# Hybrid decoder layer: inverse products one to three issued in a row, and convolution steps moved into the recurrence

## What is computed

```python
h = einsum('btd,dc->btc', x, w_in)
qa, ka, va, za, ba, aa, qb, kb, vb, zb = split(h, offsets)
ya = _deltanet_group(qa, ka, va, za, ba, aa, conv_w, a_log, dt_bias, norm_w)
yb = _swa_group(qb, kb, vb, zb, sinks)
y = einsum('btc,cd->btd', concatenate([ya, yb]), w_out)
x = layernorm(2 ** 0.25 * x + y) * ln_g + ln_b
```

## Time and profile before

| | |
|---|---|
| median of 3 runs | 1091.87 us (1090.0 to 1093.45) |
| the profiled execution | 1090.27 us, its span 1088.5 us |
| TensorE matmuls busy | 1064.2 us, 98% of the span |
| TensorE weight loads busy | 846.5 us, 78% |
| VectorE busy | 688.7 us, 63% |
| ScalarE busy | 532.7 us, 49% |
| GpSimd busy | 115.9 us, 11% |
| mean granted TensorE clock | 0.999 |
| HBM read and written | 138.22 and 44.07 MB |

### The profile page before, as it was taken

The page is one execution under the profiler, slowest core; times in us unless marked ns, Lnnn a source line. Parts: engine busy times, 40 slices in busy tenths (PEclk is TensorE's granted clock), DMA queues, the critical chain, the costliest instruction groups (busy, mean ns, idle before and its releaser), DMA issues.

```text
span 1088.5 us, 19513 instructions
## 1 busy us (share of the span) xinstructions
PE 1064.2 (98%) x7212; PEld 846.5 (78%) x7212; DVE 688.7 (63%) x2081; ACT 532.7 (49%) x1557; POOL 115.9 (11%) x152
## 2 busy tenths in 40 slices
PE   7999999999999999999999999999999999999997
PEld 5877787778778787777887878787787878787885
DVE  5285959584665747576365665757537575758565
ACT  4557675754636454363354535435344555564300
POOL 3413132134100000020000000002000000002210
PEclk9999999999999999999999999999999999999999
DMA  8967475665553626253562551715454343622432
GB/s 282 315 209 262 163 274 195 243 208 183 201 205 109 237 73 235 87 185 98 175 228 93 165 215 46 265 49 185 132 179 157 126 157 128 215 73 63 137 116 77
DMA packets 58430, 183.55 MB, mean 169 GB/s; under 512 B 8480, under 2 KB 21216, under 8 KB 45024
## 3 DMA queue, kind: packets, MB, share of 16 engines
q1 hardware_dynamic: 58192, 182.05, 48.7%
q10 hardware_dynamic: 144, 0.26, 0.1%
HBM read 138.22 MB, written 44.07 MB: 167 GB/s over the span
## 4 chain that ended last, share of the span: by engine, by line
PE 65%; DVE 6%; DMA 2%; issue 1%; ACT 0%; SPq 0%; DVEq 0%
PE bank L849 33%; PE bank L900 10%; PE bank L1137 4%; PE bank L957 2%; PE bank L990 2%; PE bank L972 2%; PE bank L1107 1%; PE bank L1120 1%; PE bank L1117 1%; PE bank L1121 1%; DVE y_cols L1797 1%; DVE y_step L1793 1%; PE bank L1030 1%; PE bank L1045 1%; PE bank L1115 1%
## 5 line engine op out<-in xcount | busy, mean ns | idle before, releaser
L849 PE MATMUL bank<-xr,w 128*128 128x512 f32 x2496 | 653.9, 405 | 7.4 <-DVE xr L1534 7.4
L849 PEld LDWEIGHTS bank<-xr,w 128*128 128x128 f32 x2496 | 449.8, 189 | 101.7 <-issue 9.8
L900 PE MATMUL bank<-wo,y_split 128*128 128x512 f32 x432 | 114.4, 404 | 0.0
L900 PEld LDWEIGHTS bank<-wo,y_split 128*128 128x128 f32 x432 | 77.0, 189 | 14.6 <-issue 0.7
L1582 DVE SCALAR_TENSOR_TENSOR kq<-conv_in,convw_all,kq 128x512 f32<-128x512 f32 x96 | 77.3, 806 | 7.8 <-ACT conv_in L1191 5.8
L1487 ACT ACTIVATE o_scaled<-bank 128x128 f32<-128x128 f32 x64 | 17.7, 277 | 124.5 <-PE bank L1121 124.3
L1353 ACT ACTIVATE score<-score,neg_max 128x256 f32<-128x256 f32 (+1 forms) x128 | 62.7, 493 | 29.0 <-DVE neg_max L1759 29.0
L1919 DVE TENSOR_SCALAR steps<-bank,nb_rk 128x128 f32<-128x128 f32 x64 | 22.3, 348 | 63.9 <-PE bank L1117 63.9
L1922 DVE SCALAR_TENSOR_TENSOR state<-state,cols_all,bank 128x128 f32<-128x128 f32 x64 | 22.2, 347 | 63.2 <-PE bank L1120 63.2
L1793 DVE TENSOR_TENSOR y_step<-blocks,y_cols 128x60 f32<-128x60 f32 (+14 forms) x240 | 50.3, 210 | 12.1 <-DMA blocks<-n_spill 3.3
L783 POOL TENSOR_TENSOR xr<-y_tile,xr 128x256 fp32r<-128x256 f32 x8 | 6.0, 774 | 455.1 <-ACT xr L1172 455.1
(11 more groups left out here) (217 smaller groups left out, 1628.3 us busy)
## 6 DMA issues: line engine op xcount, KB each, us to landing
w<-w_split SPq DMA_DIRECT2D x78, 1024.0 KB, 5.4
w_split<-w SPq DMA_DIRECT2D x26, 1024.0 KB, 5.1
blocks<-n_spill SPq DMA_DIRECT2D x32, 256.0 KB
y_spill<-y_out SPq DMA_DIRECT2D x30, 256.0 KB, 5.8
x_tile<-w_in SPq DMA_DIRECT2D x13, 512.0 KB, 6.1
y_tile<-w_in SPq DMA_DIRECT2D x12, 512.0 KB, 6.4
y_tile<-y_spill SPq DMA_DIRECT2D x12, 512.0 KB, 6.1
x_tile<-x SPq DMA_DIRECT2D x12, 512.0 KB, 3.9
```

What stands on the lines that cost most here:

```text
L849: ins = nc.tensor.matmul(bank[JOBS[at].bank][:], w[:, turn % 3, wp, k, :], xr[:, xp, k], start=(step == 0), stop=(step == 3 * KT - 1))
L900: ins = nc.tensor.matmul(bank[JOBS[at].bank][:], y_place(t)[:, yp, k], wo[:, k, wp, half * UNIT:(half + 1) * UNIT], start=(step == 0), sto ...
```

## The change

On TensorE, product 1 comes directly behind the dense steps of `p16`; then follow the second scores, product 2, the first values and product 3, with no dense steps between them. `Places` loses `p32`, and the others move: `p16` by +0.3 of a level, `y16` (still used by VectorE and ScalarE) to 1.6 levels, `y32` to 2.8. A level is 4 to 7 dense steps.

On VectorE, the transpose of product 2 stands directly behind the copy of product 1. Behind it come `gate_b`, the copies into `t32`, the finished output jobs, the weight or `split_y` and only then the maxima. On ScalarE the copies of products 2 and 3 stand before all exponentials of the second half.

The convolution is counted in single taps, 9 a slot, where it was counted in halves. From slot 3 on (`n >= AH - 1`) none is done ahead of the base inverses; one tap may follow the maxima, q's three taps are completed after `divide`, and the other six are handed out one at a time in the recurrence of chunks 0 and 1, behind `resid`, behind `v_new` and behind `state`. `slopes` moves to chunk 2 there. In slots 0 to 2 what `convs` does ahead of the base inverses stays, and the rest comes in one block after `divide` as before.

```diff
-        self.p16, self.y16, self.p32, self.y32, self.p64 = (first + level * a for a in range(5))
+        self.p16, self.y16, self.y32, self.p64 = (first + level * a for a in (0.3, 1.6, 2.8, 4))
...
                 fill_to(n, at.turns0)
                 turns(n, 0)
                 fill_to(n, at.p16)
-                values(n, 0)
                 after(pe, t_ready, n, 1)
                 after(pe, pt_ready, n, 2)
                 quads_of(lambda c, rows: nc.tensor.matmul(quad_place(bank[6], rows, c), n_t[rows, c, rows], t0[rows, c],
                                                           start=True, stop=True)).then_inc(inv_done.sem, 1)
                 scores(n, 1)
-                fill_to(n, at.y16)
                 after(pe, r_ready, n, 1)
                 after(pe, v_tok_ready, n, CH)
                 quads_of(lambda c, rows: nc.tensor.matmul(quad_place(bank[4], rows, c), r16[rows, c], y0[rows, c],
                                                           start=True, stop=True)).then_inc(inv_done.sem, 1)
-                fill_to(n, at.p32)
+                values(n, 0)
                 after(pe, t_ready, n, 2)
                 pairs_of(lambda c, one, two: nc.tensor.matmul(quad_place(bank[6], two, c), n_t[one, c, two], t16[one, c],
                                                               start=True, stop=True)).then_inc(inv_done.sem, 1)
...
                 after_jobs(n, at.p16)
                 after(act, t_ready, n, 2)
                 nc.scalar.activation(y16, quad_tiles(bank[4]), ACT.Copy).then_inc(inv_copied.sem, 1)
-                weights(n, 1, (0,))
+                take(p32, quad_tiles(bank[6]), 3)
+                weights(n, 1)
                 after_jobs(n, at.y16)
-                take(p32, quad_tiles(bank[6]), 3)
-                weights(n, 1, (1,))
                 after(act, inv_copied, n, 1)
                 for b in range(4):
                     rows = slice(b * QUAD, (b + 1) * QUAD)
                     nc.scalar.activation(y_inv[rows, :, rows], y16[rows], ACT.Copy)
                 if n == SLOTS - 1:
                     round_y(11)
-                after_jobs(n, at.p32)
+                after_jobs(n, at.y16)
...
-            def conv(m, c, half):
+            def conv(m, c, step):
...
-                if half == 0:
+                if step == 0:
                     after(dve, raw_copied, m, c + 1)
                     after(dve, tail_put, m, 1)
-                for step in (0,) if half == 0 else (1, 2):
-                    if step > 0:
-                        after(dve, conv_step, m, 2 * c + step)
-                    ins = nc.vector.scalar_tensor_tensor(acc, conv_in[:, c, step:step + UNIT],
-                                                         convw_all[:, i, c, step:step + 1], acc, ALU.mult, ALU.add)
-                    ins.then_inc(conv_step.sem if step < CONV - 2 else conv_ready.sem, 1)
-                if c == 2 and half == 1:
+                else:
+                    after(dve, conv_step, m, 2 * c + step)
+                ins = nc.vector.scalar_tensor_tensor(acc, conv_in[:, c, step:step + UNIT],
+                                                     convw_all[:, i, c, step:step + 1], acc, ALU.mult, ALU.add)
+                ins.then_inc(conv_step.sem if step < CONV - 2 else conv_ready.sem, 1)
+                if c == 2 and step == CONV - 2:
                     nc.vector.tensor_copy(tails[:, i], conv_in[:, :, UNIT:]).then_inc(tail_saved.sem, 1)
                     if m < SLOTS - 1:
...
-            def convs(n, f, most=6):
-
-                while conv_place[0] < 6 * SLOTS and most > 0:
-                    m, part = divmod(conv_place[0], 6)
-                    c, half = divmod(part, 2)
+            def convs(n, f, most=9):
+
+                while conv_place[0] < 9 * SLOTS and most > 0:
+                    m, part = divmod(conv_place[0], 9)
+                    c, step = divmod(part, 3)
                     if JOBS[JOB_AT["qkv"[c], m]].end > n + f + 1e-6:
                         return
-                    conv(m, c, half)
+                    conv(m, c, step)
                     conv_place[0] += 1
                     most -= 1
+
+            def conv_gap(n, f):
+
+                if n >= AH - 1:
+                    convs(n, f, 1)
...
-                convs(n, 0.2)
+                if n < AH - 1:
+                    convs(n, 0.2)
                 after_jobs(n, at.base)
                 if n == SLOTS - 1:
                     split_y(9)
                 base_inverses(n)
-                after_jobs(n, at.p16)
+                if n < AH - 1:
+                    after_jobs(n, at.p16)
                 after(dve, inv_done, n, 1)
                 nc.vector.copy_predicated(r16[:], lower16[:].rearrange("p b c -> p (b c)").unsqueeze(1).to_broadcast([P, CH, QUAD]),
                                           quad_tiles(bank[6])).then_inc(r_ready.sem, 1)
-                gate_b(n, 0)
-                if t is not None and i < AH - 1:
-                    split_y(t)
-                else:
-                    convs(n, 0.34, 1)
-                maxima(n, 1)
                 after(dve, inv_done, n, 2)
                 nc.vector.transpose(t16, quad_tiles(bank[4])).then_inc(t_ready.sem, 1)
+                gate_b(n, 0)
                 after(dve, t_ready, n, 2)
                 for b in range(2):
                     rows = slice(b * QUAD, (b + 1) * QUAD)
                     nc.vector.tensor_copy(t32[rows, :, rows], t16[rows])
+                after_jobs(n, at.p16)
+                if n < AH - 1:
+                    weight_rest(n, "k")
+                if t is not None and i < AH - 1:
+                    split_y(t)
+                maxima(n, 1)
+                if n >= AH - 1 and (t is None or i == AH - 1):
+                    convs(n, 0.34, 1)
                 if t is not None and i == AH - 1:
                     normalise(n, at.y16)
-                if n < AH - 1:
-                    weight_rest(n, "k")
-                after_jobs(n, at.p32)
+                after_jobs(n, at.y16)
                 if n < AH - 1:
                     convs(n, 0.34, 1)
                 after(dve, inv_done, n, 4)
                 nc.vector.transpose(t32[QUAD:HALF, :, 0:QUAD], quad_tiles(bank[5])[0:QUAD]).then_inc(t_ready.sem, 1)
                 divide(n, 1)
-                if n < SLOTS - 1:
+                if n < AH - 1:
                     slopes(n + 1)
                 if i == AH - 1 and s < SBS - 1:
                     after_jobs(n, JOBS[JOB_AT["bT", s + 1]].end - n)
                 if n == SLOTS - 1:
                     split_y(10)
                     split_y(11)
-                convs(n, at.p32)
+                convs(n, at.y16, 9 if n < AH - 1 else max(0, 9 * (n + 1) + 3 - conv_place[0]))
                 after_jobs(n, at.step0)
...
                     nc.vector.scalar_tensor_tensor(resid, bank[4][:, 0:P], col(EG)[:, one], v_tok[:, c], ALU.mult, ALU.subtract)\
                         .then_inc(resid_ready.sem, 1)
                     after_jobs(n, at.chunk(c, 1 / 3))
+                    conv_gap(n, at.p64 if c == 0 else at.chunk(c - 1))
                     after(dve, tr_done, n, c + 1)
                     nc.vector.tensor_scalar(v_new, bank[6][:, 0:P], nb_rk[:, one], None, ALU.mult).then_inc(v_new_ready.sem, 1)
                     after_jobs(n, at.chunk(c, 2 / 3))
+                    conv_gap(n, at.p64 if c == 0 else at.chunk(c - 1))
                     after(dve, kv_done, n, c + 1)
                     nc.vector.scalar_tensor_tensor(state[:, i], state[:, i], col(EGT)[:, one], bank[4][:, P:2 * P],
                                                    ALU.mult, ALU.add).then_inc(state_ready.sem, 1)
                     if n == SLOTS - 1 and c < 3:
                         split_y(12 + c)
                     after_jobs(n, at.chunk(c, 0.8))
-                    if c < 3:
-                        convs(n, (at.p64, at.chunk(0), 1)[c], 1 if n == AH - 1 and c < 2 else 6)
+                    if n < AH - 1:
+                        if c < 3:
+                            convs(n, (at.p64, at.chunk(0), 1)[c])
+                    elif c < 2:
+                        convs(n, (at.p64, at.chunk(0))[c], 1)
+                    elif c == 2:
+                        convs(n, 1)
+                        if n < SLOTS - 1:
+                            slopes(n + 1)
                     if c == CH - 1:
                         if t is not None and i == AH - 2:
                             split_y(t + 1)
```

## The result

The changed kernel takes 1098.94 us, median of six runs (1097.53 to 1104.37). The kernel before, run beside it on the same chip, takes 1091.64 us (1090.0 to 1095.61). The ratio is 1.008, with a 95% interval of 1.0059 to 1.0101: slower by 0.8%. The profiled execution took 1097.64 us with a span of 1095.9 us, 7.4 us more than the span before.

What follows compares the result with a forecast made beforehand. TensorE, 98% busy in matmuls, was taken as the bound. Terms -7.1 + 3.3 + 0.6 + 1.1 + 3.1 + 3.9 + 2.4 = +7.3 us gave 1097.6 from the profiled 1090.27, 1099 against the runs' median; 8-in-10 range 1091 to 1103.5.

Steps and rivals of the forecast that it cites:

- Seams: TensorE between products 1 and 4: two dense runs gone as runs, 0.22 us each, saving 0.44 us a slot, 7.1 in 16.
- Product 1's waits: Slots 0 to 3, 7, 11, 12: product 1 comes earlier but `t0` no sooner, so 3.3 us given back; bounds 0 and 4.5.
- `turns(n, 1)`: Slots 4, 5, 8, 9, 12 to 14: later second-half attention on VectorE uses up the slack; some 0.1 us each, 0.6 in all.
- `split_y` in slots 6 and 10: The o0 job starts five dense steps behind product 3 and needs `split_y`, which ends later: 2 x 0.55 = 1.1 us.
- Slots 0 to 2: VectorE, the tight engine there, idles and makes `resid` and L1117 late: 1.05 us each, 3.1 in all; ends 1.5 and 5.
- the third idle time: Slots 0 to 2: VectorE idle 0.9 us ahead of `divide`, as the weight's low part stands before the maxima.
- Chunk 1's tap: Slots 4, 5, 6, 8, 9, 10: a tap between `add_half` and `v_new` costs 6 x 0.75 = 4.5 us, net 3.9.
- Slot 15: The `after_jobs` of `p16` now stands before the maxima, delaying `split_y(10)` and chunk 1's `resid`: 2.4 us; ends 0 and 3.5.

## Why the prediction was right, and where it wasn't

The total was forecast at 1099 and came to 1098.94. The terms, in the prediction's order:

- **Seams, -0.44 us a slot.** Measured -0.46 and -0.43 in slots 13 and 14. By the Trainium skill ("TensorEngine Tiling (Array Packing)", Key Properties), read as in the prediction, only the two removed runs count; the trace agrees. The 0.22 us was read too finely: 1.60 and 1.36 us differ by 0.24, which would leave 0.16. The changed kernel's runs of 13 and 7 steps, 3.17 and 1.81 us to the next product, give 0.227 a step and 0.22 on top, so the figure stands.
- **Product 1's waits, +3.3.** Over all seven slots the gap ahead of product 1, over its smallest, grew from 4.4 to 8.4 us: +4.0. The listed row went to 7.9, forecast 7. Slot 3 is most of the difference: its gap grew by 0.93 us where 0.35 was forecast, and slot 12's by 1.0 where 0.8 was. Slot 3's moves between executions: in the kernel with slot 15's job moved, which is the same there, it grew by just 0.35.
- **`turns(n, 1)`, +0.6.** Seven waits of 0.11 to 0.13 us: 0.9.
- **`split_y` in slots 6 and 10, +1.1.** Two pauses of 0.65 us at the o0 job's start: 1.3.
- **Slots 0 to 2.** The net was right, +0.95 forecast against 0.82 to 0.98, and undoing the order gives all of it back. The place was not. The prediction put it all at L1117. There the wait, now L1115, is only some 0.5 us. The largest new one is product 5's for `t`, 0.76 us a slot, which the prediction doesn't name, and the second turns, which had waited 0.3 us in the kernel before, wait no more. VectorE in slot 0:

```profile
84.37 0.65 DVE L1763 TENSOR_TENSOR sink_in<-neg_max,pair_all 128x4 f32<-128x4 f32 x1
84.94 1.30 DVE L1578 SCALAR_TENSOR_TENSOR kq<-conv_in,convw_all,kq 128x512 f32<-128x512 f32 x1
86.27 0.30 DVE L1901 STREAM_TRANSPOSE t<-bank 32x128 f32<-32x128 f32 x1
86.65 0.16 DVE L1768 TENSOR_TENSOR denom<-row_sum,sink_exp 128x4 f32<-128x4 f32 x1
```

  VectorE idles between the answers (1.15 us) and ahead of `gate_b` (0.46), as forecast, but not ahead of `divide`, whose first instruction is the last row. Behind 1.6 us of idle time stand the weight's low part, the maxima and a tap, and then `t`: it starts 8.30 us behind product 1, 7.35 before, while product 5 is due as early as before (7.9 us). The step that failed is the third idle time, "and ahead of `divide`": the prediction went from the maxima straight to `divide` and passed over the answer in between.
- **Chunk 1's tap, +3.9.** +3.64 in `kv`'s waits, -0.64 from `tr` in slots 6 and 10: 3.0. The mechanism is shown by moving one line. A tap cost 0.67 us and not 0.75, as starts are 0.65 to 0.67 apart there; and slot 8 had waited 0.53 us already, so it paid only 0.31.
- **Slot 15, +2.4 beside the seams.** Measured 2.72 + 0.44 = 3.2. The wait for the weight, forecast to double, more than tripled, 0.81 to 2.64. The term is made of +1.83 from this wait, +0.6 from products 4 and 5 and +0.75 from `tr` in chunk 1. Here the account was incomplete: for the wait the prediction blamed the job of `p16` alone, 1.25 us. Putting it back took away 0.96 of the 1.83; the other 0.87, read from rows above, is TensorE's earlier arrival by the two dense runs that it is spared, and a split that GpSimd's work now slows. The term also moves between executions: in the profile of the kernel with `split_y` between the answers, which is the same in slot 15, the slot is 1.8 us longer and not 2.7, with a wait of 0.24 at `tr`. `divide` and the split in the changed kernel:

```profile
1008.74 2.81 DVE L1775 TENSOR_SCALAR score<-score,denom_inv 128x256 f32<-128x256 f32 x4
1011.46 1.74 DVE L1723 TENSOR_TENSOR w<-y_tile,w 128x1024 fp32r<-128x1024 f32 x1
```

The measured terms add to about 8 us; the slots' sum is 7.1 and the prologue 0.3. The difference is mostly slot 4's wait for `q_in`, 0.4 us less in this execution. That the total hit within 0.1 us is luck at this level: terms were off by up to 0.9 in both directions, and executions of the changed kernel spread over 7 us.

The rule of the Trainium skill ("Perfetto Trace Analysis", Optimizing Scalar/DVE Operations), that smaller pieces may let work finish sooner, was weighed as false for chunk 1. With the tap on the right side of the wait the traces agree with it: some 2.6 us over five slots against the taps in blocks.

Left open: how often an execution of the changed kernel meets the lower clock in slot 12 or 15. Its two longest executions (1103.18 and 1104.37 us) have mean clocks of 0.994 and 0.995 against 0.997 to 0.999 in the three shortest, but only the profiled execution shows where. What lets the clock fall behind one wait and not behind another of the same length is open too. Slots 3, 4, 7, 11 and 14, which wait for transfers or for work behind them, also move by up to 1.3 us between profiles of kernels that are the same there, for no reason shown.

## What to carry to other kernels

In an in-order queue a filler goes ahead of the wait it is to fill, not behind the work released by it; one tap on the wrong side of `add_half`, in six slots, cost 4 us. When a product is moved earlier, look at each of its inputs in each kind of slot, and let the places differ by slot: the change cost 0.8% with one order for all, and with the tap on the right side gained 0.5% where the row was kept out of four slots and product 1 was timed in four others. Work that depends on a transfer stands between two answers that the bounding engine waits for only where the transfer is surely early: product 3 waited 0.67 us behind `split_y` in slot 9 of one kernel and 1.3 in slot 4 of another, but not in slots 6 and 10.

## What the runs showed of the hardware

A pause of TensorE can cost more than itself. Behind product 3's wait of 3.7 us in slot 5 the granted clock was 0.50 for over 5 us. How long the pause is doesn't settle it: in slot 12, behind product 1's waits of 1.85, 1.87, 2.18 and 2.25 us, the clock was 0.50 over the scores or most of them, and behind 1.97, 2.02 and 2.14 us, at the same place in other profiles, it was 1.00. Slot 15's wait of 2.64 us shows both: in the changed kernel's profile the clock behind it is 1.00 and the dense steps start 0.23 us apart; in that of the kernel with the tap first, behind the same 2.64 us, it falls to 0.50, and steps start 0.43 us apart.
